# Making the first 384 tokens' queries and keys among the last expert rows, on one core of Trainium2

## The chip, the cores and the metric

The kernel runs on one core of a Trainium2 chip. Five engines share its work and run their own instruction streams, tied together by semaphores: TensorE (PE, matmuls), VectorE (DVE), ScalarE (ACT), GpSimd (POOL), and SyncE (SP), which here only starts DMA transfers. The metric is the device time in microseconds of one execution, the median over the runs.

## What is computed

A block for 512 tokens of width 1024: a mixer of convolutions and spatial gating, then "PEER", a layer in which every token picks 16 of 16384 experts in each of 8 heads, then a gated embedding, and then two further layers, of which the first begins with gated linear attention (GLA). The part that the change touches lies between PEER and GLA:

```python
def block(args):                       # PEER, per 128 tokens
    xb, ib, gb = args
    ug = expert_u[ib]                  # gathered rows, 128 per token
    act = jax.nn.gelu(jnp.einsum("td,tkd->tk", xb, ug)) * gb
    vg = expert_v[ib]
    return jnp.einsum("tk,tkd->td", act, vg)
...
gate = jax.nn.sigmoid(rmsnorm(h, g_ple[i]) @ w_pg[i])
h = h + (p[i] @ w_pe[i]) * gate
...
proj = h @ w_in                        # GLA
q, k, v, r, glr = jnp.split(proj, [H * DK, 2 * H * DK, 2 * H * DK + H * DV,
                                   2 * H * DK + 2 * H * DV], axis=-1)
q = q.reshape(B, S, H, DK) * (DK ** -0.5)
log_a = jax.nn.log_sigmoid((glr @ w_gate + b_gate).astype(jnp.float32)) / GLA_TAU
```

H is 4, DK is 128 and DV is 256, so q and k are 512 channels each, v and r 1024. All of it is fp32, and each step of PEER for one token needs the token's own rows alone, while GLA runs over the tokens in order.

## The kernel before

**Expert rows.** The 512 tokens are four tiles of 128 tokens, and each tile has 8 heads: 32 groups (n = 0 to 31), each with 16 rows (k = 0 to 15). A "row" is a gather: for 128 tokens one expert's 1024 values each, 0.5 MB. For group n POOL issues, in turn, the U row (n + 1, k) and the V row (n, k), by an indirect DMA each (line 1631). DVE multiplies a U row with the tokens and sums it (line 2711). PE adds a V row into two PSUM banks: two matmuls with a diagonal matrix of coefficients as weights and 512 columns (`v_row`, line 1022). The table `ON_DVE` says which V rows DVE adds instead, by one multiply and add of 128x1024 (`summed_row`, lines 2742 and 2745). In the last group these are the first `SUMMED` rows. The last group has no U rows behind it, so its 16 V rows are gathered one after another.

**Early work.** The first 384 tokens (three tiles; `early`) are through PEER when the last tile's groups (24 to 31) begin. So PE makes their further steps in between, written out by row in the loop over n and k: the embedding, the gate, the norm, and from row (28, 12) on the GLA values. `v_items` gives three matmuls (128x256) to each of 32 rows, up to (30, 11): 12 products ("items") of eight matmuls, which `early_values` (line 1177) puts into one of four PSUM banks, and which ACT copies out (line 2042). Their weights are "units" of 1 MB (256 columns of a weight matrix, for all 1024 inputs), which SP loads into the two slots of `wring`, each when its slot's last user is done.

**The last 128 tokens** (`late`) follow when the last V row is added. A chain of short steps on DVE, ACT and PE makes their sum, norm, gate and next norm: `last_turn` (line 1225), the gate products (line 1257), `last_turn` twice, and then the products of the first query unit. That unit is split: its columns of early tokens are made by `first_q(j, early_q)` (line 1238, 128x384), j = 0 before the first `last_turn` and j = 1 ahead of the second; the late columns behind. Then come the decay (lines 1276 and 1281), the second query unit and both key units for all 512 tokens (`unit`, line 677), the values of the late tokens (line 1290), and eight rounds of a small attention product (line 1302, 32 matmul records of 16 columns) and one product of r (line 1311). Ahead of each attention product DVE forms differences of decays (`k_diff`, line 2876), ACT their exponentials (line 2155), and DVE multiplies these by the keys (line 2890).

**POOL beside it.** When the second and third `last_turn` and the late norm are through, POOL begins `ada(1)`: 12 units of 1 MB of the modulation weights, each loaded into `aslot1` (line 1550), multiplied by the condition vector and added up (lines 1563 to 1567). The slot lies where the transposed keys `kwt` of the attention will stand. So ACT waits for `ada_done` ahead of the copy that writes `kwt` (line 2166), after the eighth round and the transposes of the keys (line 1320), and ahead of everything that follows: the state loop (lines 1334 to 1341), the output projection and the two feed-forward layers.

```python
            need("ada_done", 1)
            for h in range(GLA_H):
                need("kw_t", h + 1)
                inc(e.activation(kwt[:, 4 * h:4 * h + 4, :], ps[:, 4 + h, :].rearrange("p (a k) -> p a k", a=4), ACT.Copy),
                    "kw_tok")
```

Of the kernel before, what the change touches and what calls it, by code (L numbers as in the profile page):

```python
# [19 lines left out]
P = 128  # L20
EPS = 1e-6

T = 512
# [12 lines left out]
SUMMED = 6  # L36
# [70 lines left out]
def build(nc, A, out):  # L107
    with ExitStack() as ctx:
# [161 lines left out]
        gv_early = arena[:, pT_end - 3 * D:pT_end].rearrange("p (t k) -> p t k", t=3)  # L270
# [10 lines left out]
        last_dg = keysT  # L281
        dump = qT[:, 0:2, :].rearrange("p a k -> p (a k)")
        dump_g = ring_low[:, 6, :]
        sums_l = qT[:, 2, :]
# [6 lines left out]
        ON_DVE = {26: (1, 3, 6, 8, 11, 13), 27: (2, 6, 10, 14), 28: (11, 14), 29: (1, 3, 6, 8, 11, 13), 30: (1, 3, 6, 8, 11, 13),  # L291
# [4 lines left out]
        VALUES_SEEN = {28: range(0, 1), 29: range(1, 6), 30: range(6, 12)}  # L296
# [74 lines left out]

        R = Region()
        gq = R.take(GLA_H, T)
        gk = R.take(GLA_H, T)
# [11 lines left out]
        whi_go = rounded_pair("whi_go", (gb_at, R.at), DC * UNIT)  # L386
        qsub = R.take(GLA_H, T)
        amat = R.take(GLA_G, P)
        aslot1 = arena[:, pT_end - 3 * D - 2 * DC * UNIT:pT_end - 3 * D].rearrange("p (a k n) -> p a k n", a=2, k=DC)
        assert R.at <= pT_end - 3 * D - 2 * DC * UNIT  # L390
        R = Region(pT_end - 3 * D - 2 * DC * UNIT)
        kwt = R.take(GLA_G, P)
        state = R.take(GLA_H, GLA_DV)
        R = Region(pT_end)
        reset = R.take(T)
        keep = R.take(P)
        elast = R.take(GLA_G)
# [69 lines left out]
        def _(e):  # L467
# [90 lines left out]
            e.wait_ge(S["gv_t"], FROM["gv_t"] + 9)  # L558
# [14 lines left out]
            e.wait_ge(S["gv_t"], FROM["gv_t"] + 12)  # L573
# [54 lines left out]
        def _(e):  # L628
# [539 lines left out]
            def early_values(item, k):  # L1168

                u, t = divmod(item, 3)  # L1170
                if k == 0:
                    if t == 0:
# [57 lines left out]
            early_q, late_q = slice(0, EARLY), slice(EARLY, T)  # L1230
# [4 lines left out]
            def first_q(j, cols):  # L1235

                for k in range(DC):
                    mm = e.matmul(ps[:, q_bank + j, cols], w_q0[:, k, j * P:(j + 1) * P], nT[:, k, cols],
# [30 lines left out]
            for j in range(2):  # L1269
                first_q(j, late_q)  # L1270
# [1813 lines left out]
```

## Time and profile before

| | us |
|---|---|
| median of 3 runs | 3039.62 |
| lowest and highest | 3019.64 to 3051.65 |
| the profiled execution, its own time | 3029.9 |
| its span in the trace | 3028.2 |
| groups 0 to 31 with their rows end at | 1747 |
| late tokens, GLA, up to the state loop | 1747 to 1960 |

The trace holds one execution. Times in it count from the start of its span, and the 1.7 us between span and time lie around it. A fp32 matmul stands in the trace as two MATMUL records, so a product of eight matmuls counts as x16. A record's own duration is longer than the distance to the next one, since matmuls overlap; a stretch's length divided by its count is the cost of one.

### The profile page before, as it was taken

How to read it: one execution, taken by the hardware profiler on the slowest of the kernel's cores; microseconds unless marked ns; L12 is line 12 of the kernel's file. 1: busy time of each engine (PE TensorE's matmuls, PEld its weight loads, DVE VectorE, ACT ScalarE, POOL GpSimd, SP SyncE). 2: the span in 40 equal slices, each digit the busy share in tenths (PEclk: the TensorE clock that was granted, in tenths of full speed). 3: DMA queues.
4: the chain of work that ended last, by engine and by line, in shares of the span. 5: the costliest groups of instructions: out<-in, count | busy, mean ns of one | idle time of the engine just before them, and what ended most of it. 6: DMA issues, size and time to landing. Idle time of an engine off the chain costs nothing. (4 is left out here: it accounts for less than half of the span.)

```text
span 3028.2 us, 26603 instructions
## 1 busy us (share of the span) xinstructions
PE 2637.7 (87%) x8945; PEld 1591.3 (53%) x8945; DVE 1517.2 (50%) x3312; ACT 612.9 (20%) x1291; POOL 1671.4 (55%) x1273
## 2 busy tenths in 40 slices
PE   8995998758768777777987898999999999999999
PEld 7653443323223222223434555678888854678887
DVE  6864656556565666555676545444415534221121
ACT  2221222112121122112221132321110123221100
POOL 5304666666666666666675648546665401156664
PEclk9997999979999999998998999999999999999999
DMA  6347999999999999999999955125436320122232
GB/s 204 112 134 291 369 385 347 368 355 367 370 369 385 359 387 362 368 373 371 356 402 338 384 164 183 66 98 179 148 99 216 115 69 28 44 91 95 95 105 85
DMA packets 329451, 729.49 MB, mean 241 GB/s; under 512 B 24981, under 2 KB 191811, under 8 KB 329347
## 3 DMA queue, kind: packets, MB, share of 16 engines
q0 software_dynamic: 150720, 549.52, 47.7%
q1 hardware_dynamic: 141186, 140.94, 14.5%
q10 hardware_dynamic: 37440, 37.75, 3.9%
q8 instruction: 53, 0.87, 0.1%
q14 instruction: 52, 0.42, 0.0%
HBM read 726.03 MB, written 2.10 MB: 240 GB/s over the span
## 5 line engine op out<-in xcount | busy, mean ns | idle before, releaser
L2711 DVE CUSTOM_DVE_ANT_0 arena<-arena,ps 128x1024 f32<-128x1024 f32 x508 | 613.9, 1216 | 261.8 <-DMA arena<-in_expert_u_dram,arena 170.3
L1022 PE MATMUL ps<-arena 128*128 128x512 f32 x1152 | 575.5, 630 | 176.6 <-DMA arena<-in_expert_v_dram,arena 80.8
L1631 POOL DMA_INDIRECT arena<-in_expert_u_dram,arena x508 | 482.7, 950 | 291.9 <-issue 148.1
L1022 PEld LDWEIGHTS ps<-arena 128*128 128x128 f32 x1152 | 215.7, 198 | 503.0 <-issue 318.7
L1022 PE MATMUL ps<-work,arena 128*128 128x512 f32 x776 | 385.9, 630 | 87.0 <-DMA work<-in_expert_v_dram,arena 46.8
L1631 POOL DMA_INDIRECT arena<-in_expert_v_dram,arena x308 | 290.8, 944 | 181.7 <-issue 89.3
L1599 POOL TENSOR_TENSOR wlo<-wring,whi_f 128x2048 fp32r<-128x2048 f32 (+1 forms) x60 | 302.9, 5048 | 22.6 <-DVE n_lo L2851 11.9
L1022 PEld LDWEIGHTS ps<-work,arena 128*128 128x128 f32 x776 | 145.0, 197 | 308.1 <-issue 188.6
L1593 POOL TENSOR_SCALAR whi_f<-wring 128x2048 fp32r<-128x2048 f32 (+1 forms) x60 | 125.4, 2090 | 285.8 <-DMA wring<-in_ffn_w_in_dram 169.3
L723 PE MATMUL ps<-n_hi,wlo 128*128 128x512 f32 x1024 | 255.1, 391 | 0.1
L1631 POOL DMA_INDIRECT work<-in_expert_v_dram,arena x204 | 195.7, 959 | 87.7 <-issue 51.2
L723 PEld LDWEIGHTS ps<-n_hi,wlo 128*128 128x128 f32 x1024 | 191.7, 188 | 42.8 <-POOL wlo L1599 1.4
L2944 DVE TENSOR_TENSOR arena<-ps,arena 128x512 f32 (+1 forms) x44 | 30.4, 692 | 353.3 <-PE ps L727 353.3
L719 PE MATMUL ps<-n_hi,whi_f 128*128 128x512 f32 x704 | 170.0, 394 | 6.0 <-ACT n_hi L1775 6.0
L727 PE MATMUL ps<-n_lo,whi_f 128*128 128x512 f32 x704 | 174.8, 390 | 0.3 <-DVE n_lo L2851 0.3
L1939 ACT ACTIVATE arena<-ident,arena 128x128 f32<-128x128 f32 x482 | 148.2, 388 | 119.4 <-remote 53.9
L719 PEld LDWEIGHTS ps<-n_hi,whi_f 128*128 128x128 f32 x704 | 134.2, 191 | 35.8 <-issue 7.6
L727 PEld LDWEIGHTS ps<-n_lo,whi_f 128*128 128x128 f32 x704 | 132.2, 188 | 28.9 <-DVE n_lo L2851 1.7
L2397 DVE SCALAR_TENSOR_TENSOR hT<-ps,mod,hT 128x512 f32<-128x512 f32 x32 | 24.0, 751 | 221.4 <-PE ps L727 221.3
L1593 POOL TENSOR_SCALAR whi_m<-wring 128x2048 fp32r<-128x2048 f32 x7 | 13.8, 1966 | 186.4 <-DMA wring<-in_mla_w_out_dram 177.9
L986 PE MATMUL ps<-nT,wring 128*128 128x512 f32 x192 | 90.2, 594 | 0.0
L723 PE MATMUL ps<-hid_h,wlo 128*128 128x512 f32 x352 | 85.1, 389 | 0.0
(400 smaller groups left out, 3557.3 us busy)
## 6 DMA issues: line engine op xcount, KB each, us to landing
wring<-in_ffn_w_in_dram SPq DMA_DIRECT2D x44, 1024.0 KB
arena<-in_ada_w_dram ACTq DMA_DIRECT2D x24, 1024.0 KB, 5.5
wring<-in_ffn_w_out_dram SPq DMA_DIRECT2D x16, 1408.0 KB
wring<-in_gla_w_in_dram SPq DMA_DIRECT2D x16, 1024.0 KB
arena<-in_ada_w_dram POOLq DMA_DIRECT2D x12, 1024.0 KB, 5.9
work<-in_ada_w_dram ACTq DMA_DIRECT2D x12, 1024.0 KB, 5.3
wring<-in_w_in_dram SPq DMA_DIRECT2D x9, 1024.0 KB
wring<-in_w_q_dram SPq DMA_DIRECT2D x8, 1024.0 KB
```

The costliest lines, as they stand in the source:

```text
L719: e.matmul(banks[j], wh[:, k, cols[j]], hi(k), start=(start and k == 0), stop=False)
L723: e.matmul(banks[j], wl[:, k, cols[j]], hi(k), start=False, stop=False)
L727: mm = e.matmul(banks[j], wh[:, k, cols[j]], lo(k), start=False, stop=(stop and k == kc - 1))
L986: mm = e.matmul(ps[:, j, :], w[:, k, j * P:(j + 1) * P], nrhs(k), start=(k == 0), stop=(k == DC - 1))
L1022: mm = e.matmul(ps[:, 6 + q, :], diag[:, k, :], slot_of(row_)[:, q * 512:(q + 1) * 512], start=first, stop=last)
L1593: e.tensor_scalar(hi, w, 1.0, 0.0, ALU.mult, ALU.add).then_inc(w_split.sem, 1)
L1599: e.tensor_tensor(wlo[:, q, 0:kc * UNIT], w, hi.bitcast(F32), ALU.subtract).then_inc(S["w_lo"], 1)
L1631: e.indirect_dma_start(slot_of(row_), None, expert_u if kind == "u" else expert_v, bass.IndirectOffsetOnAxis(ap=idx_flat[:, n * TOPK + k:n ...
L1939: inc(e.activation(diag[:, k, :], ident[:], ACT.Copy, scale=coef[:, n % 2, k:k + 1]), "diag_ready")
L2397: ins = e.scalar_tensor_tensor(out=dst, in0=bank, scalar=mod[:, gate + m:gate + m + 1], in1=dst, op0=ALU.mult, op1=ALU.add)
L2711: inc(e.tensor_tensor_reduce(slot_of(row_), slot_of(row_), ps[:, 4:6, :].rearrange("p a k -> p (a k)"), 1.0, 0.0, ALU.mult, ALU.add, dots[ ...
L2944: e.tensor_tensor(hid[:, bass.ds(i * 2 + j, 1), :].rearrange("p a k -> p (a k)"), ps[:, 2 + j, :], gsil[:, j, :], ALU.mult).then_inc(raw.s ...
```

## The change

Eight more products join the items: both query units and both key units of the early tokens, 128x384 each, eight matmuls a product, items 12 to 19. They are made four matmuls to a row on the 16 rows from (30, 12) to (31, 11). So they fill the end of group 30 and most of the last group. `first_q(j, early_q)` goes, and the second query unit and the key units are made for the late 128 columns alone afterwards. SP therefore loads the four units twice: once for the items, and once more for the late columns (4 MB more). Four more V rows go to DVE: group 30 has the eight even rows on DVE instead of six rows, and the last group's first eight rows instead of six. `gq` and `gk` move to where the keys of the scores stood. DVE clears the attention banks ahead of a wait, not after it, and puts the differences of the first two rounds, and their products, ahead of the decay to the end of the tile (`ew_ready`) and its two products. From the third round on it makes `k_diff` and the product of the same round, one behind the other. ACT copies the first late value ahead of the exponentials.

```diff
-SUMMED = 6
+SUMMED = 8
...
-        ON_DVE = {26: (1, 3, 6, 8, 11, 13), 27: (2, 6, 10, 14), 28: (11, 14), 29: (1, 3, 6, 8, 11, 13), 30: (1, 3, 6, 8, 11, 13),
+        ON_DVE = {26: (1, 3, 6, 8, 11, 13), 27: (2, 6, 10, 14), 28: (11, 14), 29: (1, 3, 6, 8, 11, 13), 30: range(0, TOPK, 2),
                   UNITS - 1: range(SUMMED)}
...
-        VALUES_SEEN = {28: range(0, 1), 29: range(1, 6), 30: range(6, 12)}
+        VALUES_SEEN = {28: range(0, 1), 29: range(1, 6), 30: range(6, 12), 31: range(12, 20)}
...
             at = TOPK * (n - V_FIRST) + k - V_ROW
-            return [divmod(3 * at + q, DC) for q in range(3)] if 0 <= at < 32 else []
+            if at < 32:
+                return [divmod(3 * at + q, DC) for q in range(3)] if at >= 0 else []
+            return [divmod(96 + 4 * (at - 32) + q, DC) for q in range(4)] if at < 48 else []
...
-            e.wait_ge(S["gv_t"], FROM["gv_t"] + 9)
+            for q, past in enumerate((9, 12, 14, 16)):
+                e.wait_ge(S["gv_t"], FROM["gv_t"] + past)
+                next_unit(gla_in, q * UNIT, DC, UNIT)
+            e.wait_ge(S["gv_t"], FROM["gv_t"] + 18)
             near = ("v", UNITS - 1, TOPK - 3)
             e.wait_ge(sem_of(near), landed_in(near))
             next_unit(gla_in, 0, DC, UNIT)
...
-                mm = e.matmul(ps[:, (2 + item) % 4, 0:UNIT], nT[:, k, t * P:(t + 1) * P],
-                              held[3][:, k, :], start=(k == 0), stop=(k == DC - 1))
+                if is_value:
+                    mm = e.matmul(ps[:, (2 + item) % 4, 0:UNIT], nT[:, k, t * P:(t + 1) * P],
+                                  held[3][:, k, :], start=(k == 0), stop=(k == DC - 1))
+                else:
+                    mm = e.matmul(ps[:, (2 + item) % 4, early], held[3][:, k, j * P:(j + 1) * P], nT[:, k, early],
+                                  start=(k == 0), stop=(k == DC - 1))
...
-            need("gv_taken", 12)
-            first_q(0, early_q)
+            need("gv_taken", 20)
...
-            first_q(1, early_q)
...
             for q in range(3):
-                unit(DC, nrhs, act)
+                w = slot(DC)
+                for j in range(2):
+                    b = 2 * ((st["u"] - 1) % 2) + j
+                    e.wait_ge(act.sem, act.value(3))
+                    for k in range(DC):
+                        mm = e.matmul(ps[:, b, late], w[:, k, j * P:(j + 1) * P], nT[:, k, late], start=(k == 0),
+                                      stop=(k == DC - 1))
+                    inc(mm, "chunk_done")
+                    act.add()
...
+            own(e.memset(ps[:, 4:8, :], 0.0))
             need("glog_l", 1)
             need("consts", 3)
             own(e.tensor_tensor(gtmp, gb, gtmp2, ALU.subtract))
-            own(e.memset(ps[:, 4:8, :], 0.0))
...
-            for i in range(8):
-                n = 16 * (i + 1)
-                need("dk_exp", i + 1)
-                own(e.tensor_tensor(kd_g(i % 2)[:, :, 0:n], kd_g(i % 2)[:, :, 0:n], gkg[:, :, 0:n], ALU.mult), "k_sub")
-                if i + 2 < 8:
-                    k_diff(i + 2)
+            k_scaled(0)
+            k_scaled(1)
+            own(e.tensor_tensor(gsubs(gtmp2), gbg[:, :, P - 1:P].to_broadcast([P, GLA_G, P]), gbg, ALU.subtract), "ew_ready")
+            for i in range(2, 8):
+                k_diff(i)
+                k_scaled(i)
+                if i == 2:
+                    need("ew_exp", 3)
+                    own(e.tensor_tensor(gq, gq, gtmp, ALU.mult), "ew_done")
+                    own(e.tensor_tensor(gtmp2, gtmp2, gk, ALU.mult), "kw_ready")
```

PE's program at the end of the V rows stands so before. L1022 is a V row (x2 matmuls a row), L1177 an item of the values, L1238 the early query product, L1225 the first `last_turn`; "work" and "arena" are the slots that the row landed in:

```order
421 L1177 MATMUL ps<-wring,nT 128x256 x6
422 L1022 MATMUL ps<-arena 128x512 x2
423 L1177 MATMUL ps<-wring,nT 128x256 x3
424 L1022 MATMUL ps<-arena 128x512 x2
425 L1177 MATMUL ps<-wring,nT 128x256 x6
426 L1022 MATMUL ps<-work,arena 128x512 x6
427 L1022 MATMUL ps<-arena 128x512 x12
428 L1022 MATMUL ps<-work,arena 128x512 x8
429 L1238 MATMUL ps<-nT,wring 128x384 x8
430 L1225 MATMUL ps<-arena 128x128 x8
```

And so after (L1025 is the V row, L1185 the query and key items, L1233 `last_turn`), from the last three matmuls of the values on:

```order
423 L1182 MATMUL ps<-wring,nT 128x256 x3
424 L1185 MATMUL ps<-nT,wring 128x384 x4
425 L1025 MATMUL ps<-work,arena 128x512 x2
426 L1185 MATMUL ps<-nT,wring 128x384 x8
427 L1025 MATMUL ps<-work,arena 128x512 x2
428 L1185 MATMUL ps<-nT,wring 128x384 x36
429 L1025 MATMUL ps<-arena 128x512 x2
430 L1185 MATMUL ps<-nT,wring 128x384 x4
...
436 L1185 MATMUL ps<-nT,wring 128x384 x4
437 L1025 MATMUL ps<-work,arena 128x512 x8
438 L1233 MATMUL ps<-arena 128x128 x8
```

Of the rows from (30, 12) on, 13 stood on PE and 10 do now, and 64 matmuls of 384 columns are among and between them; the early query product ahead of `last_turn` is gone.

PE's products between the decay (L1281) and the attention rounds (L1302) before, where L677 is the second query unit and the key units:

```order
434 L1238 MATMUL ps<-nT,wring 128x128 x16
435 L1276 MATMUL ps<-nT,arena 16x512 x8
436 L1281 MATMUL ps<-arena 128x512 x4
437 L677 MATMUL ps<-nT,wring 128x512 x48
438 L1290 MATMUL ps<-wring,nT 128x256 x32
439 L1302 MATMUL ps<-arena,work 16x16 x16
```

The same place after:

```order
441 L1245 MATMUL ps<-nT,wring 128x128 x16
442 L1280 MATMUL ps<-nT,arena 16x512 x8
443 L1285 MATMUL ps<-arena 128x512 x4
444 L1293 MATMUL ps<-nT,wring 128x128 x48
445 L1302 MATMUL ps<-wring,nT 128x256 x32
446 L1314 MATMUL ps<-arena,work 16x16 x16
```

The 48 matmuls stay at their place and lose three quarters of their columns.

## Rows read from the trace of the kernel before

**Rows 1.** The page: the span.

```profile
span 3028.2 us, 26603 instructions
```

**Rows 2.** Chain that ended last, 1560 to 1960: start us, us, what.

```profile
1688.88 1.72 PE ps L1022 x4
...
1747.05 5.16 PE ps L1238 x16
...
1753.99 14.05 PE ps L1257 x64
...
1777.51 3.58 PE ps L1238 x32
...
1787.34 41.22 PE ps L677 x96
1828.71 5.31 DMA wring<-in_gla_w_in_dram
```

**Rows 3.** Timeline of PE: start, us, line, form, [idle before, releaser].

```profile
1711.97 1.88 PE L1022 MATMUL ps<-work,arena 128*128 128x512 f32 x4
1714.69 1.98 PE L1022 MATMUL ps<-work,arena 128*128 128x512 f32 x4 [0.85 <-DMA work<-in_expert_v_dram,arena]
...
1727.15 13.04 PE L1022 MATMUL ps<-arena 128*128 128x512 f32 x24 [7.94 <-DMA arena<-in_expert_v_dram,arena]
...
1752.05 1.95 PE L1225 MATMUL ps<-arena 128*128 128x128 f32 x16
...
1773.67 3.84 PE L1225 MATMUL ps<-arena 128*128 128x128 f32 x32 [0.48 <-DVE arena L2829]
...
1849.80 0.96 PE L1302 MATMUL ps<-arena,work 128*16 128x16 f32 x32 [0.53 <-ACT arena L2147]
...
1938.71 1.97 PE L1320 MATMUL ps<-ident,arena 128*128 128x128 f32 x16 [0.69 <-ACT arena L2158]
```

**Rows 4.** Timeline of DVE: a V row, the sum, the diagonal, the decay's steps.

```profile
1714.54 1.28 DVE L2745 SCALAR_TENSOR_TENSOR arena<-work,arena 128x1024 f32<-128x1024 f32 x1
...
1747.16 1.29 DVE L2809 TENSOR_TENSOR arena<-ps,arena 128x512 f32<-128x512 f32 x2 [19.12 <-PE ps L1022]
1750.28 0.28 DVE L2811 TENSOR_SCALAR arena<-ident,arena 128x128 f32<-128x128 f32 x1 [1.84 <-ACT arena L2081]
...
1792.10 2.43 DVE L2861 TENSOR_TENSOR arena<-arena 128x2048 f32<-128x2048 f32 x1 [3.12 <-ACT arena L2124]
...
1796.83 9.20 DVE L2864 TENSOR_TENSOR_SCAN arena<-arena 128x512 f32<-128x512 f32 x4
...
1831.10 2.29 DVE L2883 TENSOR_TENSOR arena<-arena 128x2048 f32<-128x2048 f32 x1 [11.82 <-ACT arena L2135]
```

**Rows 5.** Timeline of POOL: a late gather, then `ada(1)` and the split behind it.

```profile
1724.05 0.99 POOL L1631 DMA_INDIRECT arena<-in_expert_v_dram,arena  x1 [0.30 <-issue]
...
1778.12 1.88 POOL L1550 DMA_DIRECT2D arena<-in_ada_w_dram  x2 [28.77 <-PE ps L1225]
1784.04 3.60 POOL L1563 TENSOR_TENSOR arena<-arena,cT 128x2048 f32<-128x2048 f32 x1 [4.05 <-DMA arena<-in_ada_w_dram]
...
1794.03 3.96 POOL L1563 TENSOR_TENSOR arena<-arena,cT 128x2048 f32<-128x2048 f32 x1
...
1926.94 0.72 POOL L1567 TENSOR_TENSOR arena<-arena 128x256 f32<-128x256 f32 x1
```

**Rows 6.** POOL by line, 1778 to 1928: busy us, mean ns, idle before.

```profile
L1566 POOL TENSOR_TENSOR arena<-arena 128x1024 f32<-128x1024 f32 (+1 forms) x24 | 64.6, 2691 | 1.9
```

**Rows 7.** Timeline of ACT: the copy behind the wait for `ada_done`.

```profile
1939.46 2.06 ACT L2166 ACTIVATE arena<-ps 128x512 f32<-128x512 f32 x4 [0.81 <-PE ps L1320]
```

**Rows 8.** Stretches: us, busy PE, PEld, DVE, ACT, POOL, granted PE clock, DMA share, GB/s.

```profile
1700.00:1711.00 11.00, 11.00 (x41) 7.43 (x40) 7.44 (x11) 0.77 (x2) 8.56 (x9) 1.00 1.02 397
...
1719.00:1727.00 8.00, 0.20 (x1) 0.00 (x0) 7.03 (x7) 1.34 (x5) 6.17 (x7) 0.68 0.98 372
1727.00:1747.00 20.00, 19.85 (x41) 8.74 (x42) 1.03 (x1) 2.09 (x3) 5.28 (x6) 0.87 1.02 367
```

More of the change, by code:

```diff
@@ L369, in sem_of @@
             return row_landed[places[row][0]]
+        gq, gk = [x.rearrange("p (h k) -> p h k", h=GLA_H) for x in (
+            keysT[:, :, :].rearrange("p a k -> p (a k)"), qT[:, :, :].rearrange("p a k -> p (a k)"))]
         R = Region()
-        gq = R.take(GLA_H, T)
-        gk = R.take(GLA_H, T)
+        qsub = R.take(GLA_H, T)
+        amat = R.take(GLA_G, P)
+        reset = amat[:, 0:4, :].rearrange("p a k -> p (a k)")
         gv_late = R.take(D)
@@ L2124, in _ @@
             inc(e.activation(gtmp2, gtmp2, ACT.Ln, bias=1.0), "glog_l")
-            q_or_k = (copy_to(gq, scale=GLA_DK ** -0.5), copy_to(gk))
-            for q in range(2):
+            for q, (dst, scale) in enumerate(((gq, GLA_DK ** -0.5), (gk, 1.0))):
                 for p in range(2):
@@ L2130, in _, with value_evac @@
                         e.wait_ge(done.sem, done.value())
-                        q_or_k[q](ps[:, 2 * (st["u"] % 2) + j, :], 2 * p + j).then_inc(evacs.sem, 1)
+                        e.activation(dst[:, 2 * p + j, late], ps[:, 2 * (st["u"] % 2) + j, late], ACT.Copy, scale=scale
+                                     ).then_inc(evacs.sem, 1)
                         evacs.add()
                     st["u"] += 1
+            def value_evac(u):
+                done.add(2)
+                e.wait_ge(done.sem, done.value())
+                e.activation(gv_late[:, u * UNIT:(u + 1) * UNIT], ps[:, 2 * (u % 2), 0:UNIT], ACT.Copy).then_inc(evacs.sem, 2)
+                evacs.add(2)
+            value_evac(0)
             need("dq_ready", 1)
@@ L2139, in _ @@
                 inc(e.activation(kd_g(i % 2)[:, :, 0:n], kd_g(i % 2)[:, :, 0:n], ACT.Exp, scale=1.0 / 16), "dk_exp")
+            for u in range(1, 4):
+                value_evac(u)
+            st["u"] += 4
             need("ew_ready", 1)
@@ L2143, in _ @@
             inc(e.activation(gtmp2, gtmp2, ACT.Exp, scale=1.0 / 16), "ew_exp")
-            for u in range(4):
-                done.add(2)
-                e.wait_ge(done.sem, done.value())
-                e.activation(gv_late[:, u * UNIT:(u + 1) * UNIT], ps[:, 2 * (u % 2), 0:UNIT], ACT.Copy).then_inc(evacs.sem, 2)
-                evacs.add(2)
-            st["u"] += 4
             for i in range(8):
@@ L2877, in k_diff, with k_scaled @@
                                     gbg[:, :, 0:n], ALU.subtract), "dk_ready")
+            def k_scaled(i):
+                n = 16 * (i + 1)
+                need("dk_exp", i + 1)
+                own(e.tensor_tensor(kd_g(i % 2)[:, :, 0:n], kd_g(i % 2)[:, :, 0:n], gkg[:, :, 0:n], ALU.mult), "k_sub")
             k_diff(0)
```

59 lines of the change are left out of this document (28 added, 31 removed).

## The prediction

> **What bounds the kernel now.** The span is 3028.2 us [rows 1], and the change acts on its stretch from 1712 to 1960. I read that stretch by its ends and asked of each what came last. The first end is that of the V rows. PE's timeline [rows 3] has row (30, 12) at 1711.97 and, after a hole of 7.94 us in which it waits for the gather of row (31, 6), the ten last rows from 1727.15 on. DVE takes the sum at 1747.16 [rows 4]. So the last rows are partly paced by gathers, partly by PE, and the hole is the only large room on PE: with the 0.85 us ahead of row (30, 14) it makes 8.8 us.
>
> The second end is the copy that ACT makes behind the wait for `ada_done`, at 1939.46 [rows 7]. Everything later in the program stands behind it. Its row says that PE's transposes released it, and these came at 1938.71 [rows 3]. But a second path ends just before: POOL begins `ada(1)` at 1778.12 and is through at 1926.94 + 0.72 = 1927.66 [rows 5], 149.5 us later. This path is 1939.46 - 1927.66 = 11.8 us early. Whoever only reads the chain sees PE alone there, and 41.22 us of its line L677 [rows 2] that the change cuts. The point of this case is that `ada(1)` starts only when the late tokens' `last_turn` is done, so all that the V rows lose goes into this path in full, and nothing that PE saves afterwards comes out of it.
>
> **V rows and items.** Before, PE needs 1747.05 - 1711.97 = 35.1 us from row (30, 12) to its first instruction behind the V rows [rows 2, 3]; 13 rows are in it. A row without a wait costs 1.72 us [rows 2], ten of them 17.2 us. One 384-column product of eight matmuls costs 5.16 us [rows 2], 0.645 us a matmul, so the 64 of the items cost 41.3 us. The stretch becomes 17.2 + 41.3 = 58.5 us. The rows of group 31 that stay on PE begin behind 44 or so of these matmuls, at about 1745, and the gather of (31, 8) was issued at 1724.05 [rows 5]; the one of (31, 6) took under six microseconds to its matmul. So no gather is waited for any more, the hole is filled, and the slower start behind it goes too (six rows in 13.04 us against 10.3 at 1.72 each, 2.7 us [rows 3]). That room is already in the difference, 58.5 - 35.1 = +23.4 us. One row fewer on PE in (30, 0) to (30, 11) gives back 1.72 us if PE is the limit there; PE is busy for all of 1700 to 1711 [rows 8]. Against it stands the load of the first query unit, 1 MB in a stretch whose DMA share is 1.02 at 397 GB/s [rows 8], so up to 1.05 / 0.397 = 2.6 us of delay for gathers. I take -1.0 for both (bounds -1.7 and +0.9). **V rows end 22.4 us later, at 1769.5**; bounds 21.7 to 24.3.
>
> Other costs there I put at nothing. The four rows that DVE takes over run at 1.28 us [rows 4] beside PE; DVE is done with the last group's rows some 20 us before PE, and if this cover were gone they would cost 2.6 us. Items 16 to 19 wait until ACT has copied items 12 to 15, which it does only behind the last group's diagonals. The hidden sum for these was there at 1717, the diagonals need row (30, 15), now at about 1724, and item 16 begins at 1735: 7 us of room. The weights of an item pair are asked for when the pair before the last is done, so 10.3 us before their use; a load took 5.31 us in the stretch behind [rows 2]. The room is 5 us a load, in a DMA that is full until the gathers end. In SP's queue the late gate weights, the GLA gate's and the second query unit stand behind these loads. They are due at 1774 and later and asked for from 1745 on, so nothing.
>
> **The late tokens.** The early query product ahead of `last_turn` (5.16 us) was cover: DVE's diagonal is there at 1750.28 + 0.28 and PE came at 1752.05 [rows 3, 4]. It gives 1.4 us, not 5.2. The second one ended just before 1773.67, where PE still waited 0.48 us for DVE [rows 3], so it gives nothing. In return PE now stands still for 3.6 us ahead of the gate products. Behind 8 us of waiting the granted clock was 0.68 and then 0.87 of full speed [rows 8], so partly at the lower of its two levels, 1.2 instead of 2.4 GHz, and six rows lost 2.7 us. I take +1.5 for the 14.05 us of gate products [rows 2] (bounds 0 and 2.7). Sum +0.1: `ada(1)` begins at 1778.12 + 22.4 + 0.1 = 1800.6.
>
> **From there to the copy, by PE.** The six products of 41.22 us become 6 x 1.79 = 10.7 us (3.58 us for two of 128 columns [rows 2]). But then PE meets others. DVE subtracts at 1792.10 [rows 4], 22.5 us later now; behind that stand 9.2 us of scans [rows 4] and, by my estimate, 12 us of differences and first products of the same kind of 128x2048 operation, so the first attention round is ready at 1838 or so. The weights, a load of 5.3 us each into two slots, allow the last late value at 1840. I put the first round at 1841, against 1849.80 [rows 3]: 9 us earlier in spite of the later start. Its eight rounds took 88.9 us up to the transposes at 1938.71. Some waits for DVE in them may go, since two rounds are ready in advance. So PE gets to the transposes at 1925 to 1930, and would give 9 to 14 us.
>
> **By POOL.** The same 12 units from 1800.6 on: 149.5 us give 1950.1. They are no shorter than 5.9 us for the first load (1778.12 to 1784.04) and twelve times 10.0 us for a unit that nothing disturbs (1784.04 to 1794.03 [rows 5]), 125.9 us, which ends at 1926.5. The 23.6 us above this come from sharing with DVE: the additions of L1566 have a mean of 2691 ns [rows 6] against 1.86 us in the first unit. DVE has the same instructions to do in both kernels, and all of them beside `ada(1)` in both. I take 149.5, bounds 138 and 160. **The copy moves from 1939.46 to 1950.1, +10.6 us.**
>
> PE then has stood still for some 20 us, and the state loop behind the copy is 19 us of small matmuls at full clock now. The nearest row is again the start behind the 7.94 us hole: 2.7 us lost. I take +2.4, bounds 0 and 5.
>
> The Trainium skill, "TensorE: Matmul & The Clock Gate", section "Loop structure matters more than you think", says that matmuls with a long wait before them run cold, and this speaks against a change that turns PE's products into waits. Rows 8 agree that the clock is lower behind the hole. By that rule both terms for the clock stand; without it the sum would be 3.9 us lower.
>
> **The sum.** 22.4 + 0.1 - 11.8 + 2.4 = +13.1 us, with 11.8 the room that POOL's path has now. The profiled execution's 3029.9 us becomes 3043.0. It is 9.7 us under the median of the three runs, and the step is the same for both: 3039.62 + 13.1, about **3052 us**.
>
> **Rivals.**
> *A, PE still ends last.* If `ada(1)` gets through in under 130 us, the copy follows PE's transposes at 1930: -9.5 us, and with a start of the V rows' end as above the time is 3030. For it: the undisturbed unit is 10.0 us. Against it: DVE's work lies closer together now, with less idle time for POOL. The same result comes if the V rows' end moves by only 11 us, because more of PE's time there is waiting than the timeline shows. Chance 0.17.
> *B, the weights come late.* Each of the units for items 14 to 19 is asked for 10.3 us ahead, while gathers fill the DMA at a share of 1.02. From a load of over 10.3 us on, the PE program waits, and each microsecond over it counts three times. At 16 us, three times the 5.31, this is 17 us, all of it in POOL's path: 3069 and, with the clock lost in the waits, up to 3075. For it: the DMA is full. Against it: gathers end at about 1740, and the value units were loaded in the same crowd without a wait that I find. Chance 0.12.
> *C, POOL is slowed more.* With DVE's work denser beside the first units, 10 more microseconds for `ada(1)`: 3062. The Trainium skill, "SBUF — State Buffer", section "Who interferes with whom", says that a VectorE instruction with two SBUF inputs and a GpSimd instruction that reads SBUF exclude each other, and that the order of issue decides who blocks. By it the 23.6 us could as well be shifted to DVE or grow; the sum above keeps the measured value. Chance 0.16.
> *D, as forecast*, 3042 to 3060: chance 0.55.
>
> **How the numbers follow.** The likeliest is D, 3052. The range takes in A's 3030 with some spread of the medians, and C, and part of B: 3026 to 3073. A measurement here can hardly tell less than 1%, 30.4 us. Slower by more than that needs over 3070, which is most of B and a tail of C: 0.10. Faster by more needs under 3009, 20 us below A, and no mechanism gives it: 0.04. Within 1%: 0.86.
>
> **What would show it.** In the profile after: PE without a hole between (30, 12) and the last row; DVE's sum at 1769 or so; POOL's first load of `ada(1)` at 1800; PE's transposes of the keys before 1932, and the copy behind `ada_done` near 1950, released by POOL. The prediction is wrong if the copy is again released by PE (A), or if PE's query and key items show waits for DMA (B).

## The result, and the profile after

Both kernels ran side by side on one chip. Before: 3029.63 us (median of 4 runs, 3018.82 to 3051.65). After: 3062.94 us (4 runs, 3052.73 to 3075.99). The ratio is 1.0114, 95% interval 1.0075 to 1.0153: slower by 1.1%, 33 us. The forecast of the step was +13.1 us, which is less than half of it. The time lies in the range given, in its upper part. It is only 11 us from the 3052 us of the forecast because the forecast counted from a median of 3039.62 us for the kernel before, 10 us above the 3029.63 of this comparison: luck, not insight.

The profiled execution of the changed kernel took 3063.99 us. Its page begins:

```profile
span 3062.4 us, 26783 instructions
```

The span grew by 34.2 us [rows 1]. PE's timeline (start, us, line, form, and in brackets the idle time before and its releaser; L1025 is a V row, L1182 a value product, L1185 a query or key product, L1233 `last_turn`, L1314 the first attention round, L1332 the transposes of the keys, L1346 the state loop) answers to rows 3:

```profile
1722.41 1.22 PE L1185 MATMUL ps<-nT,wring 128*128 128x384 f32 x3
...
1736.44 2.74 PE L1185 MATMUL ps<-nT,wring 128*128 128x384 f32 x8
1746.94 22.72 PE L1185 MATMUL ps<-nT,wring 128*128 128x384 f32 x64 [7.75 <-DMA wring<-in_gla_w_in_dram]
1769.50 1.88 PE L1025 MATMUL ps<-arena 128*128 128x512 f32 x4
...
1786.68 7.03 PE L1025 MATMUL ps<-work,arena 128*128 128x512 f32 x16
1797.37 2.81 PE L1233 MATMUL ps<-arena 128*128 128x128 f32 x16 [3.66 <-DVE arena L2835]
...
1820.51 6.31 PE L1233 MATMUL ps<-arena 128*128 128x128 f32 x32 [5.64 <-DVE arena L2853]
...
1871.98 0.96 PE L1314 MATMUL ps<-arena,work 128*16 128x16 f32 x32 [0.53 <-ACT arena L2157]
...
1955.14 1.97 PE L1332 MATMUL ps<-ident,arena 128*128 128x128 f32 x16 [0.69 <-ACT arena L2182]
1974.13 1.19 PE L1346 MATMUL ps<-arena 128*128 128x128 f32 x4 [17.03 <-ACT arena L2190]
```

The gather for row (31, 8) is no longer waited for, but PE still stands still ahead of item 14: 7.75 us, and now for the weights of the second query unit. Behind the keys' transposes it stands still for 17 us. The rest of the chain is in the timelines of DVE (the sum behind the V rows), POOL (the first and last instruction of `ada(1)`) and ACT (the copy behind `ada_done`), which answer to rows 4, 5 and 7:

```profile
1793.82 1.29 DVE L2833 TENSOR_TENSOR arena<-ps,arena 128x512 f32<-128x512 f32 x2 [50.02 <-PE ps L1025]
...
1827.43 1.88 POOL L1562 DMA_DIRECT2D arena<-in_ada_w_dram  x2 [31.41 <-PE ps L1233]
...
1972.59 0.72 POOL L1579 TENSOR_TENSOR arena<-arena 128x256 f32<-128x256 f32 x1
...
1973.39 2.07 ACT L2190 ACTIVATE arena<-ps 128x512 f32<-128x512 f32 x4 [18.31 <-POOLq L1589]
```

The releaser of the copy has changed from PE [rows 7] to POOL's queue, as the prediction said, and 0.08 us after POOL's last addition. Read as a sum from one profile to the other:

| term | predicted | measured | from |
|---|---|---|---|
| V rows' end (DVE's sum) | +22.4 | +46.7 | 1747.16 to 1793.82 |
| late tokens, up to the start of `ada(1)` | +0.1 | +2.7 | 30.96 to 33.61 behind that |
| `ada(1)` itself | 0 | -3.7 | 149.54 to 145.88 |
| room of POOL's path used up | -11.8 | -11.7 | 11.80 to 0.08 |
| copy behind `ada_done` | +10.6 | +33.9 | 1939.46 to 1973.39 |
| everything behind it | +2.4 | +0.3 | the difference to 34.2 |

The first term is off by 24 us, the next two by 2.6 and -3.7. The windows (us, busy time of PE, PEld, DVE, ACT and POOL, granted clock of PE, DMA share, GB/s) show its surroundings, and in the last two lines the restart of PE behind the copy:

```profile
1722.00:1739.00 17.00, 15.73 (x43) 7.32 (x41) 8.34 (x11) 3.80 (x12) 11.65 (x12) 1.00 1.03 401
1739.00:1747.00 8.00, 0.24 (x2) 0.06 (x1) 4.77 (x4) 0.49 (x1) 0.83 (x1) 0.80 1.04 387
1747.00:1755.00 8.00, 8.00 (x20) 4.61 (x21) 0.00 (x0) 0.49 (x1) 0.00 (x0) 0.77 0.15 46
...
1955.00:1973.00 18.00, 1.97 (x16) 1.73 (x16) 0.00 (x0) 0.08 (x1) 16.76 (x10) 0.70 0.35 117
1973.00:1996.00 23.00, 21.39 (x145) 20.26 (x145) 5.54 (x12) 13.85 (x24) 8.60 (x4) 0.86 0.01 2
```

Here the wait ends where the DMA comes out of its full stretch: share 1.04 up to 1747, 0.15 from there on. It need not: with the copy freed (below) the same load lands at 1598.67, while the share stays at 1.03 until 1610.

### The profile page after: what moved, and what is told of

Same layout as the page of the kernel before. It is cut to its first block, busy times and chain, and to the rows that moved or that the text cites. A ratio compares the mean times of both kernels' runs of the same rounds, so it can differ in the third digit from the quotient of the medians.

```text
span 3062.4 us, 26783 instructions
## 1 busy us (share of the span) xinstructions
PE 2636.5 (86%) x9025; PEld 1600.3 (52%) x9025; DVE 1514.7 (49%) x3316; ACT 613.4 (20%) x1295; POOL 1666.9 (54%) x1273
## 4 chain that ended last, share of the span: by engine, by line
PE 37%; POOL 5%; DVE 3%; issue 2%; DMA 1%; ACT 1%; another core or an unknown queue 1%; POOLq 0%; DVEq 0%; SPq 0%; ACTq 0%
PE ps L730 9%; PE ps L726 9%; PE ps L722 8%; POOL arena L1578 2%; PE ps L1025 2%; POOL arena L1575 1%; PE ps L1182 1%; PE ps L1185 1%; PE ps L1430 1%; DMA wring<-in_ffn_w_in_dram 1%; PE ps L1469 1%; PE ps L1488 1%; DVE arena L2735 1%; PE ps L921 1%; PE ps L1468 1%
## 5 line engine op out<-in xcount | busy, mean ns | idle before, releaser
L1025 PE MATMUL ps<-arena 128*128 128x512 f32 x1144 | 566.2, 625 | 169.4 <-DMA arena<-in_expert_v_dram,arena 74.7
L1025 PE MATMUL ps<-work,arena 128*128 128x512 f32 x768 | 388.4, 639 | 103.1 <-issue 60.3
L1025 PEld LDWEIGHTS ps<-arena 128*128 128x128 f32 x1144 | 212.8, 196 | 489.5 <-issue 314.7
L1025 PEld LDWEIGHTS ps<-work,arena 128*128 128x128 f32 x768 | 145.2, 200 | 327.3 <-issue 218.6
```

The lines of the kernel that those rows point to most:

```text
L1025: mm = e.matmul(ps[:, 6 + q, :], diag[:, k, :], slot_of(row_)[:, q * 512:(q + 1) * 512], start=first, stop=last)
```

## The experiments

Twelve kernels ran in three groups, each on another chip. On all three the kernel before takes 2896 us or so instead of 3030 (2895.87, 2895.46 and 2897.17 us, medians of 31, 29 and 34 runs). The first group is the changed kernel with the copy freed, the one with small loads, two units early, and the kernel before with eight rows on DVE. The second is the changed kernel itself, the one with both edits, one unit early with the copy freed, and no unit early. The third is the kernel before with the copy freed and the three with the old order. Ratios are each against the runs of the kernel before on the same chip. Starts are compared between single profiles, often of two of these three chips, and such starts scatter: POOL issues the gather of V row (30, 0), ahead of every changed row, between 1532.1 and 1538.9. The changed kernel is 1.0081 there (1.0051 to 1.0111), 2921.53 us.

| kernel | ratio, 95% | V rows' end | `ada(1)` ends | keys' transposes | copy | its releaser |
|---|---|---|---|---|---|---|
| before, copy freed | 1.000, 0.998 to 1.002 | 1617.36 | 1794.51 | 1799.20 | 1799.89 | PE |
| changed | 1.008, 1.005 to 1.011 | 1648.12 | 1827.65 | 1809.54 | 1827.73 | POOL |
| changed, copy freed | 1.003, 1.001 to 1.005 | 1646.43 | 1826.77 | 1808.56 | 1809.25 | PE |
| changed, small loads | 1.006, 1.004 to 1.008 | 1640.01 | 1819.30 | 1801.00 | 1819.38 | POOL |
| changed, both | 1.001, 0.999 to 1.003 | 1640.88 | 1820.02 | 1809.98 | 1810.67 | PE |
| changed, copy freed, old order | 1.006, 1.004 to 1.008 | 1648.97 | 1830.24 | 1819.84 | 1820.53 | PE |
| two units early | 1.003, 1.000 to 1.005 | 1625.26 | 1806.20 | 1808.91 | 1809.67 | PE |
| two, freed, old order | 1.001, 0.999 to 1.003 | 1628.37 | 1810.68 | 1808.67 | 1809.36 | PE |
| one unit early, freed | 0.999, 0.997 to 1.001 | 1619.78 | 1800.86 | 1808.07 | 1808.76 | PE |
| one, freed, old order | 1.002, 1.000 to 1.004 | 1619.88 | 1802.64 | 1818.73 | 1819.42 | PE |
| no unit early | 1.003, 1.001 to 1.005 | 1614.74 | 1793.80 | 1810.11 | 1810.87 | PE |
| before, eight rows on DVE | 0.998, 0.996 to 1.001 | 1611.87 | 1789.92 | 1799.68 | 1800.43 | PE |

### Is it the wait for ada_done? The freed copy

The transposed keys and the state get places that `ada(1)` doesn't use, and the wait goes:

```diff
-        kwt = R.take(GLA_G, P)
-        state = R.take(GLA_H, GLA_DV)
+        kwt = gk.rearrange("p h (t k) -> p (h t) k", k=P)
+        state = gtmp[:, 0:2, :].rearrange("p a (b v) -> p (a b) v", v=GLA_DV)
...
-            need("ada_done", 1)
             for h in range(GLA_H):
                 need("kw_t"
```

> The changed kernel, with the transposed keys and the state put where the keys and a spent temporary stood, so that ACT's copy no longer waits for ada_done. All of the computation is done. Theory (POOL's path from the V rows' end sets the copy): the copy follows PE's transposes, which came at 1955.1 in the changed kernel, in place of 1973.4, and PE's products of ada(1) behind the state loop find it just done. So 17 us less than the changed kernel's 3063: 3046. The work of POOL, 146 us, stays. Rival (the copy's wait is only the last of several, and POOL is needed at once for the split of the output weights): the wait appears again behind the state loop, and the time stays within 4 us of 3063.

> The kernel before with the copy free of ada_done (transposed keys in gk's place, the state in gtmp's), nothing else. Theory: PE released the copy there, 11.8 us behind the end of ada(1), so freeing it gives nothing: 0.999 to 1.001, and the gain of the same edit in the changed kernel (16.8 us) is the wait that the change made. Rival: the freed copy is worth something by itself, which part of the gain would then be: 0.997 or less.

> The changed kernel once more, beside the others of this call, so that each can be set against it on one chip. Both theories: 1.008 to 1.014 of the kernel before; V rows' end some 55 us behind the last gather issue, ACT's copy released by POOL some 180 us behind that.

In the changed kernel the edit brings 1.0081 down to 1.003, in the kernel before it brings nothing (1.000). ACT's timeline, first of the changed kernel and then with the freed copy:

```profile
1827.73 2.06 ACT L2190 ACTIVATE arena<-ps 128x512 f32<-128x512 f32 x4 [18.24 <-POOLq L1589]
```

```profile
1809.25 2.07 ACT L2191 ACTIVATE arena<-ps 128x512 f32<-128x512 f32 x4 [0.75 <-PE ps L1334]
```

The idle time before the copy falls from 18.24 to 0.75 us, and the copy comes 18.5 us earlier with `ada(1)` ending within 1 us of where it did. So some 15 us of the loss are the wait that the prediction named (2921.53 against 2905.84 us). The changed kernel's copy comes 179.6 us behind the V rows' end, as expected (some 180), and the V rows end 50 us behind the last gather's issue, where 55 were expected. But 1.003 remain without the wait, which the prediction did not foresee: PE's own path has become longer as well. Its transposes come 9.4 us later than in the kernel before (1808.56 against 1799.20).

### Do the weights come late? The early loads cut

```diff
-                next_unit(gla_in, q * UNIT, DC, UNIT)
+                next_unit(gla_in, q * UNIT, DC if q == 0 else 1, UNIT if q == 0 else 16)
```

The early loads of the second query unit and of both key units bring 8 KB each instead of 1 MB. So items 14 to 19 multiply weights that are not theirs: what this kernel leaves out is the right result, and every matmul and wait stays. The kernel with both edits does the same.

> The changed kernel, in which the early loads of the second query unit and both key units are cut from 1 MB to 8 KB each. Items 14 to 19 are made with weights that are not theirs; every matmul and wait stays. Theory (a 1 MB load that is asked for late and takes 14.4 us in the crowd makes a hole of 7.75 us ahead of item 14, and the slow start behind it 2 us more): no hole, V rows end 10 us sooner than 1793.8, and with POOL's path the time is 3053. Rival (PE itself is late there, as ACT sees items 9 to 11 done 5 to 10 us after their records, and the load only shows it): the hole shrinks but PE loses the same time elsewhere, and the time stays at 3063 within 3 us.

> The changed kernel with both edits: the copy that waited for ada_done is free of it, and the early loads of the second query unit and of both key units are cut to 8 KB (items 14 to 19 multiply wrong weights; their time is what counts). Theory: the losses are ada_done's path and the late weights, and what is left is work of PE moved from one place to the other, so the copy is released by PE, 161 to 163 us behind the V rows' end, which is 44 us behind the last gather issue, and the whole is within 0.3% of the kernel before (0.997 to 1.003). Rival: the products cut later were hidden behind DVE anyway, and PE's path has only lost: then 1.005 or more even so. Second rival: the two edits share their gain (less than 4 us between this one and the freed copy alone, where the late loads alone should be worth 6).

The chain of waits of the changed kernel (start, us, what), and then of the one with the freed copy, has the load in it:

```profile
1594.17 2.60 PE ps L1185 x8
...
1596.79 16.55 DMA wring<-in_gla_w_in_dram
...
1613.38 10.59 PE ps L1185 x32
```

```profile
1580.72 17.90 DMA wring<-in_gla_w_in_dram
...
1598.67 23.59 PE ps L1187 x64
```

A load of 1 MB takes 16.55 to 17.90 us in the full DMA, against 5.31 behind it [rows 2]. The 17.90 are the second query unit's, with the copy freed. It was asked for at 1580.72, and PE was ready for it at 1594.4, 13.7 us later, since two V rows lie between; so it waits 4.23 us. The 16.55 are those of the key unit behind it, in the changed kernel. PE waits only 0.17 us for it: it was asked for at 1596.79, just before PE stood still for the unit ahead, and PE came to it 16.4 us later. With the loads cut its timeline has no hole from the first of these products to the last row:

```profile
1581.29 2.74 PE L1185 MATMUL ps<-nT,wring 128*128 128x384 f32 x8
...
1590.75 1.88 PE L1025 MATMUL ps<-work,arena 128*128 128x512 f32 x4
1592.46 23.38 PE L1185 MATMUL ps<-nT,wring 128*128 128x384 f32 x72
...
1632.87 7.03 PE L1025 MATMUL ps<-work,arena 128*128 128x512 f32 x16
```

The V rows end 58.7 us behind the first product, where the prediction had 58.5, and 22.7 us later than in the kernel before with the freed copy, where it had 22.4. So its sum for this stretch is right for a PE that waits for nothing, and late weights are what it lacks. The same stretch takes 65.3 us in the changed kernel and 65.9 with the copy freed, 6.6 and 7.2 us more. In the changed kernel 4.3 of the 6.6 are the two waits, and 2 are slower matmuls right behind the first (12.28 us for x32 against 10.3, at a granted clock of 0.59 at first). The lighter DMA is no rival for this: behind the first product PE waits for no gather in any of these profiles. In time the edit takes 0.2%, some 6 us, both from 1.0081 to 1.0059 and, with the copy freed, from 1.003 to 1.0007. Within each pair the intervals still overlap, so the size of it is rough.

With both edits 1.0007 is left, no difference that can be told: the two losses add up (0.5% and 0.2%), and behind them the products are only moved. The profiled execution with both edits doesn't show it by itself: PE reaches the transposes 169 us behind the V rows' end there and not 161 to 162, because single rounds take 10.06 and 9.91 us instead of 7.11. The granted clock is 0.74 to 0.77 in these rounds and 1.00 with the small loads alone; what lowered it is open, since PE waited for nothing just before.

### The parts: rows alone, and fewer units

> The kernel before with the table of V rows on DVE of the change (four rows more), and nothing else of it. Theory: from row (30, 12) on PE has 10 rows in place of 13, and the last ones follow their gathers; V rows end 3 us sooner and, as PE ends last in the kernel before, the time is 3 us less than before. Rival (DVE's two rows more in group 30 delay the U rows, and with them the coefficients of the last group): no gain, or 1 to 3 us more.

> The changed kernel with only the two query units early (4 items, 12 to 15, four matmuls a row to (31, 3)); the key units are made for all 512 tokens later, as before. Theory (V rows' end and POOL's path): the items are 20.6 us of PE less in the last group, so the V rows end between 1750 and 1760, by how late the second unit's load lands, against 1793.8; POOL's path ends at 1931 to 1940, and PE's at 1932 to 1940, so the time is between 3022 and 3032, about the kernel before or under it. Rival (the early products are paid on PE in full wherever they stand): the time lies half way between 3030 and 3063, at 3046.

> The freed copy, and only the first query unit made early (items 12 and 13, which lie in the hole ahead of row (30, 13)); the other three units are made later for all tokens. The unit's load is asked for ahead of the crowd, so no late weights. Theory: PE fills its 8 us hole with 10.3 us and saves 8.6 later: the same as before or up to 0.3% faster (0.996 to 1.001). Rival (items late by their signals and not by their loads): PE waits at the turn to the next unit all the same, and the time is 1.002 or more.

> The changed kernel with none of the four units made early; what is left of the change is eight rows each on DVE in the last groups and the new order of DVE and ACT in the late part. PE makes the first query unit's product for all tokens behind the late tokens' turns. Theory: V rows' end 19 us behind the last gather issue as with the eight rows alone; the new order is worth at most 3 us: 0.996 to 1.001. Rival: the new order itself costs (the late weights and values now stand behind other things), then 1.003 or more, and this would be part of the changed kernel's loss.

The first of these sets only `SUMMED = 8` and `30: range(0, TOPK, 2)` in the kernel before. The others are the changed kernel with 2, 1 or no early unit; what isn't early is made for all tokens in the place of the late columns. None of them has `first_q` ahead of the first and second `last_turn` again.

The rows alone cost nothing (0.998): the cover taken for them holds. The expected gain of 3 us can't be told from none. Two units early are 1.0025, where 3022 to 3032 us against 3030, 0.997 to 1.001, was expected; PE waits 4.27 us for the second unit's weights there too.

The hole that was to be filled is not a fixed one. PE's timeline of the rows alone, and then with one early unit:

```profile
1584.08 1.98 PE L1022 MATMUL ps<-work,arena 128*128 128x512 f32 x4 [3.13 <-DMA work<-in_expert_v_dram,arena]
1595.60 9.29 PE L1022 MATMUL ps<-arena 128*128 128x512 f32 x16 [9.54 <-DMA arena<-in_expert_v_dram,arena]
```

```profile
1595.29 2.74 PE L1188 MATMUL ps<-nT,wring 128*128 128x384 f32 x8
1602.75 10.15 PE L1028 MATMUL ps<-arena 128*128 128x512 f32 x16 [4.72 <-DMA arena<-in_expert_v_dram,arena]
```

(The second is the one with one unit, the freed copy and the old order, below.) One unit puts 10.3 us of products ahead of the same row, and the row comes 7.15 us later, with 4.72 us of waiting for its gather still there. So its gather lands later. Some of that comes without any unit: with none early, but the new layout and order, the row starts at 1598.96. That part is there before the changed rows: POOL issues the gather of V row (30, 0) at 1532.1 in the rows alone and at 1537.0 with no unit. The other 3.8 us come with the unit. POOL's last gather is issued at 1596.4 with no unit and at 1598.9 with one, though both issue that of row (30, 0) within 0.5 us, and one megabyte more in a DMA that moves 0.40 MB/us is, as an estimate, 1.05 / 0.40 = 2.6 us. The hole is not a fixed room; what is put into it brings its own bytes.

The larger reason why one unit gives 0.999 and not a gain is at the other end. Both expectations for one unit take 8.6 us as saved later, and they are not: the first query unit's early columns stand in waits of PE for DVE in the old place. From the V rows' end to the first product of the decay it is 33.8 us with these products there (the kernel before with the freed copy), and 37.8 without them (one unit, old order), where PE stands still instead and the matmuls behind are slower. Here are PE's first and second `last_turn` of the latter:

```profile
1623.43 3.75 PE L1236 MATMUL ps<-arena 128*128 128x128 f32 x16 [3.67 <-DVE arena L2838]
...
1647.76 6.43 PE L1236 MATMUL ps<-arena 128*128 128x128 f32 x32 [5.63 <-DVE arena L2856]
```

The kernel with no unit early tells the same from the other side. It has given this old place up too, and makes the whole first query unit behind the late tokens' turns:

```profile
1647.63 13.90 PE L1246 MATMUL ps<-nT,wring 128*128 128x512 f32 x32
1661.46 1.91 PE L1281 MATMUL ps<-nT,arena 128*16 128x512 f32 x16
```

The decay's first product comes 46.7 us behind the V rows' end there (1614.74 to 1661.46) and 33.9 us in the rows alone. From it to the transposes the new order then needs 148.7 us against 154.0. So the 1.003 of this kernel is not the price of the new order, as the rival had it, but, as far as the two profiles show, that of the first query unit in an uncovered place; between them the new order gives 5 us back.

### The new order, and the candidates

DVE's and ACT's late part is put back to what it was: all four late values copied behind the decays' exponentials, the difference for `ew_ready` ahead of the key differences, and all keys scaled behind `ew_done`.

```diff
-            value_evac(0)
             need("dq_ready", 1)
...
             inc(e.activation(gtmp2, gtmp2, ACT.Exp, scale=1.0 / 16), "ew_exp")
+            for u in range(4):
+                value_evac(u)
```

> The changed kernel with the freed copy, and DVE's and ACT's late part in the order of the kernel before (all four late values copied behind the decays' exponentials, the state's decays first on DVE). Its partner is the freed copy alone (1.003 of the kernel before, transposes of the keys 162.1 us behind the V rows' end). Theory: the new order takes DVE's work out of PE's later rounds, so without it PE gets to the transposes 3 to 8 us later, and the time is 1.004 to 1.006. Rival: the new order brings the late values ahead of the rounds, where PE waits for their weights twice (7.79 and 6.10 us in the kernel without early units), so without it PE is as fast or faster, and the time is 1.003 or less.

> A candidate: only the first query unit made early (10.3 us of products where the kernel with the eight rows alone waits 9.5 us for a gather), eight rows on DVE, the copy freed, and the late part of DVE and ACT in the order of the kernel before. Theory: the hole is filled at no price and 8.6 us are saved later, 0.994 to 0.998. Rival: the rows behind the hole end later anyway, because gathers and not PE pace them or because the items come at another place than the hole: 0.999 to 1.001.

> As the candidate with one unit, but both query units early. Theory: the second unit finds no hole any more, costs 10.3 us among the V rows and 4 us of waiting for its weights and gives back 8.6 later: 4 to 8 us slower than the candidate with one unit, 0.996 to 1.001. Rival: if work moved is neutral and the wait for weights is hidden by a gather that is waited for anyway, the two are within 2 us.

With all four units early the old order costs 9.7 us (2915.5 against 2905.84, on two chips; 1.0063 against 1.003). PE's timeline shows where, 12.01 us of waiting for ACT's copy of a late value:

```profile
1728.72 8.53 PE L1304 MATMUL ps<-wring,nT 128*128 128x256 f32 x32 [12.01 <-ACT arena L2159]
```

That is a little more than the 3 to 8 us expected. With one unit early the new order is the better one as well: 2893.43 us against 2907.45, 0.999 against 1.002, with intervals that just overlap, and 188.29 against 198.85 us from the V rows' end to the transposes. With two units no pair differs in the order alone (1.001 with the old order and the freed copy, 1.003 with the new order and the wait). No run shows a cost of the new order.

The expectation that two units are 4 to 8 us behind one has failed: 2899.59 against 2907.45 us, in the other direction. In the profile of the one with one unit PE needs 198.85 us from the V rows' end to the transposes, with two 180.30. Of the 18.6 us between them 8.5 lie in the query and key units, where the second unit's products are saved, as much as the V rows' end loses (1619.88 to 1628.37). Another 8.8 lie behind them. They begin with a wait of 5.34 us for weights, where the other has 0.85, and have three rounds of 9.76 to 9.93 us instead of 7.1 against two. Why these come so, I did not find. The expectation for one unit with the old order, 0.994 to 0.998, has failed as well (1.002).

The profiled executions of one kernel scatter too: that of the kernel before with the freed copy took 2885.19 us, 13 us under the median of its runs. No kernel beat the one before by what can be measured.

## Why the prediction was right in kind and wrong in one size

- **`ada(1)` sets the copy, and PE's savings don't come out of it: right.** POOL released the copy, and taking the wait out gives back 0.5% in the changed kernel and 0.0% in the one before. Shown. Its duration was taken as unchanged, 149.5 us; it was 145.88. The fear that denser work of DVE would slow it (C) did not come true: POOL's additions had a mean of 2508 ns, 2691 before [rows 6]. The 3.7 us need not be the change's: on the other chips `ada(1)` takes 146.2 us in the kernel before with the freed copy and 145.8 in the changed one. The time of 3063 us is that of C, 3062, but C is not how it came about.
- **V rows' end: the term that was mis-sized.** The prediction has +22.4 with bounds 21.7 to 24.3; it was +46.7. With the products' first start (1722.41 against the row at 1711.97 in rows 3, +10.4), the work (58.5 - 35.1 = +23.4) and the rest of the 71.4 us that the stretch took (+12.9) it is made up. In the +12.9 are 7.75 us of waiting for weights and 2.1 us of clock (22.72 us for the row x64, where four times the 5.16 us of an x16 in rows 2 is 20.6). The other 3.0 us lie ahead of the wait, from 1722.41 to 1739.2, where 13.8 us of work took 16.8. The prediction put late weights at nothing: "the room is 5 us a load", from a lead of 10.3 us and a load of 5.31 us in an empty DMA. It had the mechanism as rival B with a chance of 0.12, a load of 16 us and 17 us of delay, and it had named a wait of these products for DMA as a sign that it is wrong. That sign came. The load was 16.55 to 17.90 us on the other chips, and 14.41 on the first. The lead was off too. On the other chips PE came to the second unit 13.7 us behind the request, because of the two V rows between, on the first only 6.7 us (1732.49 to 1739.2), because the request itself came late there (last section); and load less lead gives the 4.2 and the 7.75 us of waiting. It was waited for once and not three times, since a PE that has stood still gives the next load as much more lead. The bounds should have held this: the row at hand was 5.31 us from an empty DMA, and the profile said in the same breath that the DMA was at a share of 1.02. The forecast also gave a chance of 0.10 to slower by more than 1%, and it was 1.1%.
- **The later start, +10.4, is not the change's as far as the runs show.** The two profiles are apart before any changed row: POOL issues the gather of V row (30, 0) at 1666.9 before and at 1671.8 after, 4.9 us later. Where the kernels take 2896 to 2922 us, item 12 starts at 1580.53 to 1584.26 and row (30, 12) of the kernel before with the freed copy at 1580.63, and the V rows' end moves by 30.8 us (2.2 of a later start, 22.0 of work, 6.6 of late weights and the clock behind them). On the chip of the first comparison PE's timeline has gaps without a releaser in both kernels while the DMA is full: some 9 us at 1641 to 1661 in either, and 4.4 us more at 1690 to 1697 in the changed kernel alone, of which two rows are:

```profile
1693.06 0.59 PE L1182 MATMUL ps<-wring,nT 128*128 128x256 f32 x2 [1.01 <-issue]
...
1697.28 2.35 PE L1182 MATMUL ps<-wring,nT 128*128 128x256 f32 x4 [1.61 <-issue]
```

  Of the twelve profiles on the other chips one has such a gap in this stretch, of 1.91 us, and the others have none. What PE waited for in them stays open.
- **The hole "is filled":** it was, in the sense that no gather is waited for, but only in part as a gain. The gathers come later with a unit in it (with one, 3.8 us between two profiles), and from the second unit on PE waits for weights instead.
- **Late tokens, +0.1: +2.7.** The cover came out as taken: the first `last_turn` stands 3.55 us behind DVE's sum and stood 4.89 behind it before, 1.34 us less where 1.4 was taken. The clock was under-priced, +1.5 where +4.0 was measured. The first `last_turn` and the gate products took 0.7 and 0.8 us longer (14.89 against 14.05 for the latter). The other 2.5 us are in a place that the prediction put at nothing: it saw that the second query product is cover, but not that PE now stands still for 5.64 us there. The 32 matmuls behind took 6.31 us instead of 3.84, at a granted clock of 0.59 instead of 1.00. The difference is small beside the first term.
- **PE's path to the transposes: nearly right from the V rows' end, wrong in time.** 155.5 to 160.5 us behind it predicted (1925 to 1930 from 1769.5), 161.3 measured, 191.55 before. So PE saved 30.2 us and paid 46.7. Even without `ada_done` this is a loss, 16.4 us on the first chip and 9.4 on the others, each between two profiles.
- **Clock behind the copy: right in size, and nothing in sum.** The state loop's first six groups took 5.23 us instead of 2.63, so 2.6 us more where 2.4 was taken; the granted clock was 0.70 in the stretch of waiting and 0.86 behind it. From the copy to the end of the loop 1.4 us of it are left (21.65 us against 20.24), and of the whole rest 0.3 us only. Where the other 1.1 us came back is open.

The Trainium skill, "TensorE: Matmul & The Clock Gate", section "Loop structure matters more than you think", was drawn on for the clock, and the trace agrees in the 2.6 us. The Trainium skill, "SBUF — State Buffer", section "Who interferes with whom", was drawn on for C: no run here shows more interference in the denser stretch.

## What to carry to other kernels

Moving products from a late place of PE to an early one is free only where PE waits for something that the moved work doesn't touch. Here the hole was 8 to 9 us and the products 41, so most of the delay was their own time (22.0 of 30.8 us on the other chips). They also brought 4 MB of weights into a DMA that was full of the very gathers PE was waiting for, which made one load late. And they delayed the one event, the end of the V rows, from which another engine's 146 us begin. Before work is moved ahead of an event, list what starts at that event and how much room each of these paths has; and price a load by a row from the stretch into which it is moved, not by one from behind it. Ask also what the work costs where it stands: the first query unit's early columns filled waits there, so moving them saved nothing and let the clock fall.

## What the hardware showed that I had not expected

- A load of 1 MB took 14.41, 16.55 and 17.90 us beside gathers at 400 GB/s, about three times the 5.31 us of the same load behind them.
- On the first chip ACT's copy of the last value (item 11) ran at 1732.49, though PE's timeline has the last matmul of this item at 1721.10 to 1722.56; ACT had been idle for 5.40 us and names PE as its releaser. In the kernel before the same distance was some 5 us. On the other chips it is 0.2 us (1582.84 and 1583.04). The load behind it was asked for that much later: asked for at 1722.6, its 14.41 us would have ended at 1737.0, by calculation, before PE needed it at 1739.2. So the wait of 7.75 us in the first comparison has the late request in it as well as the long load, and the small loads, which ran on another chip, don't part the two. Whether the records of the matmuls are too early or the signal was late, no run tells.
- The kernel before took 4.6% longer on one chip than on others, at a mean granted clock of 0.95 instead of 0.98, and with gaps of PE that the others don't have.
